# Gate and up of three feed-forward blocks as seven half-size products in place of eight, with the weights split in pieces of 512 words

## The reference, cut to what matters

```
def swiglu(x, w_gate, w_up, w_down):
    return (jax.nn.silu(x @ w_gate) * (x @ w_up)) @ w_down

h = h + 0.5 * swiglu(rms_norm_2(h, norm_ffn[layer, 0]), ffn_w_gate[layer, 0], ffn_w_up[layer, 0], ffn_w_down[layer, 0])
```

## Time and profile before

| | |
|---|---|
| median of 3 runs | 2825.6 us (2819.83 to 2830.66) |
| span of the profiled execution | 2823.2 us |
| TensorE busy | 2733.2 us, 97% |
| VectorE busy | 1312.7 us, 46% |
| ScalarE busy | 847.7 us, 30% |
| GpSimd busy | 562.7 us, 20% |
| DMA | 248.24 MB, 88 GB/s in the mean |

### The profile page before, as it was taken

How to read it: one execution, slowest core, us unless ns; L and a number is a source line. 1 busy time by engine, 2 the same in 40 slices (tenths; PEclk the granted TensorE clock), 3 DMA queues, 4 the chain that set the end, 5 groups by cost and what they waited for, 6 DMA issues and landing times. The chain is left out here.

```text
span 2823.2 us, 38779 instructions
## 1 busy us (share of the span) xinstructions
PE 2733.2 (97%) x16250; PEld 2191.5 (78%) x16250; DVE 1312.7 (46%) x1851; ACT 847.7 (30%) x1269; POOL 562.7 (20%) x387
## 2 busy tenths in 40 slices
PE   7999898999999999999999999999999999999998
PEld 5868755778888788888868888888888756888886
DVE  3454668453332643435455433454334566543433
ACT  3232135521212421213263221232222346421212
POOL 2000123422112230213201212122021100031202
PEclk8999989989999999999999999999999999999999
DMA  8250310123232233323203323233232240333221
GB/s 279 62 165 24 102 38 5 60 75 105 90 105 79 86 105 96 99 87 108 79 13 108 102 92 100 79 105 104 90 104 79 64 105 1 96 98 105 90 93 42
DMA packets 256942, 248.24 MB, mean 88 GB/s; under 512 B 25972, under 2 KB 252088, under 8 KB 256640
## 3 DMA queue, kind: packets, MB, share of 16 engines
q1 hardware_dynamic: 256562, 245.70, 27.8%
q10 hardware_dynamic: 206, 0.06, 0.0%
HBM read 241.52 MB, written 2.12 MB: 86 GB/s over the span
## 5 line engine op out<-in xcount | busy, mean ns | idle before, releaser
L537 DVE TENSOR_TENSOR dense_wt_lo<-ring,dense_wt_hi 128x2048 fp32r<-128x2048 f32 (+1 forms) x177 | 436.8, 2468 | 290.2 <-ACT dense_wt_hi L522 290.2
L522 ACT CAST dense_wt_hi<-ring 128x2048 fp32r<-128x2048 f32 (+1 forms) x177 | 328.1, 1854 | 758.9 <-PE bank L764 752.8
L1276 POOL TENSOR_TENSOR dense_act_hi<-dense_act,const 128x512 fp32r<-128x512 f32 x110 | 212.8, 1935 | 1307.2 <-DVE dense_act L1268 1307.2
L764 PE MATMUL bank<-feat_hi,dense_wt_hi 128*128 128x512 f32 x1344 | 414.6, 390 | 0.0
L764 PE MATMUL bank<-feat_hi,dense_wt_lo 128*128 128x512 f32 x1344 | 413.7, 389 | 0.0
L764 PE MATMUL bank<-feat_lo,dense_wt_hi 128*128 128x512 f32 x1344 | 413.7, 389 | 0.0
L764 PEld LDWEIGHTS bank<-feat_hi,dense_wt_hi 128*128 128x128 f32 x1344 | 252.3, 188 | 53.3 <-issue 1.0
L764 PEld LDWEIGHTS bank<-feat_lo,dense_wt_hi 128*128 128x128 f32 x1344 | 252.3, 188 | 52.4
L764 PEld LDWEIGHTS bank<-feat_hi,dense_wt_lo 128*128 128x128 f32 x1344 | 252.3, 188 | 52.4
L764 PE MATMUL bank<-dense_act_hi,dense_wt_hi 128*128 128x512 f32 x912 | 281.5, 390 | 1.0 <-POOL dense_act_lo L1278 0.9
L764 PE MATMUL bank<-dense_act_hi,dense_wt_lo 128*128 128x512 f32 x912 | 280.8, 389 | 0.0
(11 more groups left out here) (631 smaller groups left out, 3842.2 us busy)
## 6 DMA issues: line engine op xcount, KB each, us to landing
ring<-in_ffn_w_gate SPq DMA_DIRECT2D x44, 1024.0 KB, 5.4
ring<-in_ffn_w_up SPq DMA_DIRECT2D x44, 1024.0 KB, 5.4
ring<-in_ffn_w_down SPq DMA_DIRECT2D x32, 1024.0 KB, 5.0
ring<-in_ada_w SPq DMA_DIRECT2D x24, 1024.0 KB, 7.5
ring<-in_ffn_w_down SPq DMA_DIRECT2D x16, 768.0 KB, 4.2
...
```

What stands on the lines that cost most here:

```text
L522: self.nc.scalar.copy(self.wh[:, n % 2, 0:words], K.ring[:, n % RING, 0:words]).then_inc(K.high_done, 1)
L537: self.nc.vector.tensor_tensor(self.wl[:, n % 2, 0:words], K.ring[:, n % RING, 0:words], self.wh[:, n % 2, 0:words].bitcast(F32), ALU.subt ...
L764: lasts[m] = pe.matmul(outs[m], a, b, start=n == 0 and p == 0, stop=end and p == 2)
L1276: nc.gpsimd.tensor_tensor(ah[:, f, :], a[:, i % 2, :], K.k("ones")[:, 0:1].broadcast_to([P, T]), ALU.mult)
```

## The change

A unit is one tile of up and the same tile of gate. The weights of a unit are taken as a 2 x 2 matrix of blocks (a11, a12: up with feature tiles 0 to 3 and 4 to 7; a21, a22: gate with the same), the features as a 2 x 2 matrix (tiles 0 to 3 or 4 to 7 by tokens 0 to 255 or 256 to 511). In place of eight block products there are seven (Strassen, in Winograd's form), P1 to P7, each of four feature tiles by 256 tokens. Four sums of weight blocks are made by GpSimd in float32, partly in place in the ring (`sums_before`, `sum_first`, `sum_last`), four sums of feature blocks by GpSimd once a block (`NextOperands.pool`), and the results are put together by accumulation in PSUM and by short additions on VectorE and copies on ScalarE. A weight piece is now one block, 512 words, with six kept in `wh` and `wl` and split five ahead of TensorE. The high part of the hidden tile moves from GpSimd to ScalarE. Hidden tiles go in groups of 4, 6, 6 and 6. A unit's weights come as two DMAs with rows of 512 bytes where a chunk had one with rows of 1 KB, and a slot of the ring is given to the chunk that needs it next, in an order worked out in `Plan.place`. The output projections and the latent projection in front of and behind the blocks use the same pieces, with whole products of 512 tokens as before. The first two blocks of the program keep the old form.

```diff
+BLOCKS = 6
+LEAD = BLOCKS - 1
+BW = 4 * P
+HT = T // 2
+GROUPS = (4, 6, 6, 6)
+STARTS = (0, 4, 10, 16)
+OPERAND = {"P1": "b11", "P2": "b21", "P3": "b22", "P4": "t4", "P5": "t1", "P6": "t2", "P7": "t3"}
...
+    unit((0, "P1"), (0, "P5"), (1, "P1"), (1, "P5"), (0, "P2"), (1, "P2"), (0, "P6"), (1, "P6"), (0, "P7"), (1, "P7"),
+         (0, "P4"), (0, "P3"), (1, "P4"), (2, "P1"), (1, "P3"), (2, "P2"), (2, "P5"))
+    for u in range(2, KF - 1):
+        unit((u, "P6"), (u + 1, "P1"), (u, "P7"), (u + 1, "P2"), (u + 1, "P5"), (u, "P4"), (u, "P3"))
+        if u + 1 in STARTS:
+            g = STARTS.index(u + 1) - 1
+            n = GROUPS[g] // 2
+            for e in (0, 1):
+                for j in range(n - 1):
+                    down(g, e, j)
...
+class Blocks:
+    def __init__(self, K, st):
+        self.K, self.nc = K, K.nc
+        self.wh, self.wl = st.sb("wt_hi", [P, BLOCKS, BW], F32R), st.sb("wt_lo", [P, BLOCKS, BW], F32R)
+        self.sums = st.sb("wt_sum", [P, BW])
...
+                self.items.append({"P1": (n, part(0), None), "P2": (n, part(1), None), "P4": (n, part(3), None),
+                                   "P5": (n, self.sums[:, :], (self.s_s13, 2 * v + 1)), "P7": (n, part(2), (self.s_s13, 2 * v + 2)),
+                                   "P6": (n, part(0), (self.s_s2, v + 1)), "P3": (n, part(1), (self.s_s4, v + 1))}[p])
...
+    def high(self, act, i):
+        if i < len(self.items):
+            n, src, need = self.items[i]
+            if need:
+                act.wait_ge(*need)
+            else:
+                self.K.wait_loaded(act, n)
+            if i >= BLOCKS:
+                act.wait_ge(self.s_used, i - BLOCKS + 1)
+            self.nc.scalar.copy(self.wh[:, i % BLOCKS, :], src).then_inc(self.s_high, 1)
+    def low(self, dve, i):
+        if i < len(self.items):
+            dve.wait_ge(self.s_high, i + 1)
+            self.nc.vector.tensor_tensor(self.wl[:, i % BLOCKS, :], self.items[i][1], self.wh[:, i % BLOCKS, :].bitcast(F32),
+                                         ALU.subtract).then_inc(self.s_low, 1)
+    def sums_before(self, pool, u):
+        if u < len(self.units):
+            n, t = self.units[u][0], self.nc.gpsimd.tensor_tensor
+            a11, _, a21, a22 = (self.K.raw(n)[:, a * BW:(a + 1) * BW] for a in range(4))
+            self.K.wait_loaded(pool, n)
+            if u:
+                pool.wait_ge(self.s_low, self.units[u - 1][1][2] + 1)
+                pool.drain()
+            t(self.sums[:, :], a21, a22, ALU.add).then_inc(self.s_s13, 1)
+            pool.drain()
+            t(a21, a11, a21, ALU.subtract).then_inc(self.s_s13, 1)
+    def sum_first(self, pool, u):
+        if u < len(self.units):
+            n, (i1, _, _) = self.units[u]
+            a11 = self.K.raw(n)[:, 0:BW]
+            pool.wait_ge(self.s_low, i1 + 1)
+            pool.drain()
+            self.nc.gpsimd.tensor_tensor(a11, self.sums[:, :], a11, ALU.subtract).then_inc(self.s_s2, 1)
+    def sum_last(self, pool, u):
+        if u < len(self.units):
+            n, (_, i2, _) = self.units[u]
+            s2, a12 = (self.K.raw(n)[:, a * BW:(a + 1) * BW] for a in range(2))
+            pool.wait_ge(self.s_low, i2 + 1)
+            pool.drain()
+            self.nc.gpsimd.tensor_tensor(a12, a12, s2, ALU.subtract).then_inc(self.s_s4, 1)
+    def product(self, pe, i, out, feats, start, rows=range(4), stop=True, shared=False):
+        h, l = self.wh[:, i % BLOCKS, :], self.wl[:, i % BLOCKS, :]
+        for k in rows:
+            xh, xl = feats(k)
+            w = slice(k * P, (k + 1) * P)
+            pe.matmul(out, h[:, w], xh, start=start and k == 0, stop=False, skip_group_check=shared)
+            pe.matmul(out, h[:, w], xl, start=False, stop=False, skip_group_check=shared)
+            last = pe.matmul(out, l[:, w], xh, start=False, stop=stop and k == 3, skip_group_check=shared)
+        return last
...
+    def pool(self, pool, q):
+        t = self.nc.gpsimd.tensor_tensor
+        f, f4 = self.f[q % 2], self.f4[q % 2]
+        if q:
+            pool.wait_ge(self.s_lo, 6 * (q - 1) + 4)
+        pool.wait_ge(self.s_f, 2 * q + 1)
+        t(self.t1, f[:, HT:T], f[:, 0:HT], ALU.subtract).then_inc(self.s_t, 1)
+        pool.drain()
+        pool.wait_ge(self.s_f, 2 * q + 2)
+        t(self.t2, f4[:, HT:T], self.t1, ALU.subtract).then_inc(self.s_t, 1)
+        t(f[:, HT:T], f4[:, HT:T], f[:, HT:T], ALU.subtract).then_inc(self.s_t, 1)
+        pool.drain()
+        pool.wait_ge(self.s_lo, 6 * q + 1)
+        t(f[:, 0:HT], f4[:, 0:HT], self.t2, ALU.subtract).then_inc(self.s_t, 1)
...
+    end = [max(place[step] for step in order if step[:3] == ("down", len(GROUPS) - 1, e)) for e in range(4)]
+    tiles = lambda e: (e, e + 4) if operands else (2 * e, 2 * e + 1)
+    bank = lambda e, m: K.bank[4 + 2 * (e % 2) + m][:, :]
+    lo, hi = slice(0, HT), slice(HT, T)
+    group = lambda u: [g for g in range(len(GROUPS)) if STARTS[g] <= u][-1]
+    a = lambda u: K.bank[2 * (u % 2)][:, lo]
+    b = lambda u: K.bank[2 * (u % 2)][:, hi]
+    c = lambda u: K.bank[2 * (u % 2) + 1][:, lo]
+    scaled = {place["unit", u, "P3"] + 1: u for u in range(KF)}
+    split = {place["unit", u, "P3"] + 2: u for u in range(KF)}
...
+        def unit(n, u, p, rows=range(4)):
+            o = OPERAND[p]
+            if u < 2:
+                pe.wait_ge(now.s_lo, now.ready(o, rows[-1]))
+            if 0 in rows:
+                pe.wait_ge(B.s_low, base + n + 1)
+                if p == "P1" and u >= 2:
+                    pe.wait_ge(s_e4, u - 1)
+                elif p == "P5" and u >= 2:
+                    pe.wait_ge(s_e5, u - 1)
+                elif p == "P6":
+                    pe.wait_ge(s_e1, u + 1)
+                elif p == "P7":
+                    pe.wait_ge(s_u2, u + 1)
+                elif p in ("P4", "P3"):
+                    pe.wait_ge(s_e3, u + 1)
+            out = {"P2": b, "P5": c, "P3": c}.get(p, a)(u)
+            last = B.product(pe, base + n, out, lambda k: sec.operand(o, k), p in ("P1", "P5"), rows, shared=True)
+            if 3 in rows:
+                last.then_inc(B.s_used, 1)
...
+            B.high(act, base + n + LEAD)
+            if n == 0:
+                now.scalar_first(act, 3, prev.done)
...
+            if n in split:
+                u = split[n]
+                f = u - STARTS[group(u)]
+                act.wait_ge(s_act, u + 1)
+                nc.scalar.copy(sec.act_hi[:, f, :], sec.gate[:, u % 2, :]).then_inc(s_ah, 1)
+            if step[0] == "unit" and step[2] == "P2":
+                u = step[1]
+                if u >= 2:
+                    act.wait_ge(s_act, u - 1)
+                act.wait_ge(B.s_used, base + n + 1)
+                nc.scalar.copy(sec.up[:, u % 2, lo], b(u)).then_inc(s_b, 1)
+            if step[0] == "unit" and step[2] == "P6":
+                u = step[1]
+                if u >= 2:
+                    act.wait_ge(s_al, u - 1)
+                act.wait_ge(B.s_used, base + place["unit", u, "P5"] + 1)
+                nc.scalar.copy(sec.gate[:, u % 2, hi], c(u)).then_inc(s_c, 1)
+                act.wait_ge(B.s_used, base + n + 1)
+                if u >= 2:
+                    act.wait_ge(s_e5, u - 1)
+                nc.scalar.copy(sec.u2[:, u % 2, :], a(u)).then_inc(s_u2, 1)
+            if step[0] == "unit" and step[2] == "P3":
+                u = step[1]
+                act.wait_ge(s_gate, u + 1)
+                nc.scalar.activation(sec.gate[:, u % 2, :], sec.gate[:, u % 2, :], ACT.Silu).then_inc(s_silu, 1)
...
+            B.low(dve, base + n + LEAD)
...
+            if n in scaled:
+                u = scaled[n]
+                g = sec.gate[:, u % 2, :]
+                dve.wait_ge(s_silu, u + 1)
+                v.tensor_tensor(g, g, K.rs[:, :], ALU.mult)
+                dve.drain()
+                v.tensor_tensor(g, g, sec.up[:, u % 2, :], ALU.mult).then_inc(s_act, 1)
...
+            if step[0] == "unit":
+                u, p = step[1], step[2]
+                up, gate = sec.up[:, u % 2, :], sec.gate[:, u % 2, :]
+                if p in ("P7", "P4", "P3"):
+                    dve.wait_ge(B.s_used, base + n + 1)
+                if p == "P2":
+                    dve.wait_ge(s_b, u + 1)
+                    v.tensor_tensor(up[:, lo], a(u), up[:, lo], ALU.add).then_inc(s_e1, 1)
+                elif p == "P7":
+                    dve.wait_ge(s_c, u + 1)
+                    v.tensor_tensor(gate[:, hi], a(u), gate[:, hi], ALU.add).then_inc(s_e3, 1)
+                elif p == "P4":
+                    if u == 0:
+                        dve.wait_ge(now.s_rs, 1)
+                    v.tensor_tensor(gate[:, lo], a(u), K.rs[:, lo], ALU.mult).then_inc(s_e4, 1)
+                    dve.drain()
+                    v.tensor_tensor(gate[:, hi], gate[:, hi], K.rs[:, hi], ALU.mult).then_inc(s_gate, 1)
+                elif p == "P3":
+                    dve.wait_ge(s_u2, u + 1)
```

(40 more changed lines are left out.)

628 lines of the change are left out of this document (513 added, 115 removed).

## The result

The changed kernel takes 2921.3 us (median of 4 runs) against 2822.7 (4 runs beside it): a ratio of 1.0349, 95% interval 1.0325 to 1.0372. It is slower by some 99 us; the forecast was slower by 55, and its range ended at 2910.

The account below looks back on a forecast made before the run. TensorE's product count times spacing bound the kernel; after the change, VectorE would, through exclusion with GpSimd. Per block -17.5 (arithmetic) + 37.5 (waits) - 1.6 (present start loss) = +18.4; three: +55 on 2825.6, giving 2881 us, range 2790 to 2910.

Parts of the forecast that it names:

- slow units: Third to fifth or later units of a group, past the split lead: some 12.4 us each instead of 10.1.
- 0.120 us a product and 10.08 us a unit: TensorE in the changed blocks: 84 products of 256 columns a unit, against 10.88 us before; gain 0.80 us a unit.
- nothing for ScalarE and the DMA: In a unit, ScalarE's 6.6 us and the DMA's 6.3 fit under TensorE; DMA up to some 2 us at block starts.
- The step-through: Four engine queues stepped in order, first come, first served: cycle of 12.4 us, 8.9 us lost per group of six.
- some 110: Sign to look for: TensorE's waits in the changed blocks, in us in all, put down to VectorE and ScalarE operations.
- 2.0 us until the third operand's sum exists: At a block's start: loss while ScalarE's copy of that operand stands behind a split awaiting the first product.
- some 8.8 in the first group: First group of a block: us lost as GpSimd also queues sums of operands and squares ahead of the weights'.
- rival (2): Changed blocks: TensorE stays the bound, units stay at 10.1 us, total 2775 to 2800 us; chance 0.18.
- -52.6 + 3 x 2: Three changed blocks with TensorE as bound: arithmetic gain of 52.6 us less 2 us for each block's start.
- (4) *Heavier: Changed blocks: no unit is spared and the start is dearer, over 2910, up to 2945 us; chance 0.08.
- hold: Exclusive time of a GpSimd operation, in which VectorE's two-SBUF-input operations are shut out: 1.08 us each.
- VectorE's 7.2 us a unit: VectorE's own work in a changed unit, 4.4 us before; alone it would fit under TensorE's 10.08.

Follow-up runs that it names:

- e1: Changed kernel with GpSimd's four sums of weights per unit cut to 8 of 512 words (first sum of a section whole): 2804.7 us, ratio 0.9953.
- e7: Changed kernel with GpSimd's four sums of weights replaced by fills with zero of the same 512 words: 2807.6 us, ratio 0.9958.
- e9: Changed kernel with each GpSimd sum of weights replaced by three fills with zero, drains between: 2812.9 us, ratio 0.9986.
- e10: Changed kernel with each GpSimd sum of weights replaced by a copy of one 512-word operand: 2814.0 us, ratio 0.9990.
- e3: Changed kernel with both the sums of weights and the start's operand sums and squares cut to 8 words: 2796.3 us, ratio 0.9938.
- e2: Changed kernel with GpSimd's operand sums and squares at the blocks' starts cut to 8 words, sums of weights whole: 2898.8 us, ratio 1.0299.
- e4: Changed kernel with GpSimd making each hidden tile's low part twice, a drain between: 2943.4 us, ratio 1.0450.
- e5: Changed kernel with all four sums of weights moved from GpSimd to VectorE, each behind a drain: 2907.3 us, ratio 1.0306.
- e8: Changed kernel with the four sums of weights on VectorE at the end of a step, without drains ahead of them: 2851.5 us, ratio 1.0123.

## Why the prediction was right and wrong

**Right: the direction and, for the slow units, the mechanism.** VectorE's operations on two SBUF tiles and GpSimd's on two SBUF tiles wait for each other, whole, and this turns a gain into a loss. e1, e7, e9 and e10 leave TensorE's, ScalarE's and VectorE's work as it is and bring every unit of the groups of six to 10.08 us; e9 excludes GpSimd's lateness there. The prediction cited the Trainium skill (SBUF — State Buffer, Who interferes with whom), by which a VectorE instruction with two SBUF inputs contends with a GpSimd instruction that reads SBUF, and not with one that only writes. The sums agree with the first half (low parts of 1129 ns) and e9's fills, which only write, with the second (791). e10 does not fit the first half: its copies read SBUF, and the low parts took 808 ns where the copies beside them took 871 for 620. Here the measurement decides: a copy with one input gave way and held VectorE up little.

**Right: 0.120 us a product and 10.08 us a unit**, and nothing for ScalarE and the DMA. The first two units of each group of six run at 10.08 and 10.45. By the formula for an isolated product in the Trainium skill (TensorE: Matmul & The Clock Gate, Back-to-back issue gap) it would have been 0.109 us, an estimate; the changed kernel shows 0.120 wherever TensorE does not wait and has its full clock, so the measured figure stands.

**Right: the steady state.** The step-through gave 12.4 us a slow unit and 8.9 lost in a group of six. It is 12.68 and 9.9, the last group 7.4: 27.2 us a block where the forecast had 26.7. TensorE's waits came to 108 us in all against "some 110", on the operations named, but that they agree is in part luck: the forecast's figure was all that the stretches lose, and they lose 147 us. The waits listed leave out the small gaps around each wait, the norm's products and the products at half clock.

**Wrong: the block's start**, "2.0 us until the third operand's sum exists" and "some 8.8 in the first group". The two terms, 10.8 us a block, measured 20.0, 27.0 and 18.8 (64.6, 71.6 and 63.4 less 44.6): 33 us more in three blocks. With the 1.5 us more in the other groups that makes 90 of the 94 us by which the blocks grew, against the 55 forecast. The distances between product starts (what exceeds 0.12 us) divide the 65.8 us of the three blocks: 22.6 in waits for the last rows of features and operands; 20.6 in the wait for `up` ahead of P6 of the third unit, 6.9 in each block; 12.8 in 138 products at half clock; some 10 in the norm's products, the first two units' P6 and small gaps. The runs tell what caused them:
- The order by itself, with nothing in VectorE's way, loses 8.2 a block (e3), not 2.0: waits for `up` in P6, the features' last row, the norm's products (1.6, there before as well), products at half clock (1.8). This took 19 us from the gain of rival (2), whose "-52.6 + 3 x 2" would give -47 before its "some for the first group": e3 stands at -22.
- The sums of weights add 5.9, 7.6 and 6.4 (e2 less e3). The wait for `up` in the third unit is 5.7 us in e2 and 1.9 in e3, as in e1.
- The squares and the operands' sums add nothing in the first and third block as long as no weight sums run, 8.2 in the second (e1 less e3).
- Together they add 11.5, 18.9 and 10.7 (changed kernel less e3). The second block is dearest, probably since its operands are made while the first block's last outputs are added.

The step that failed is the stepping through the first group. I had priced the start by GpSimd's queue, as a delay of the weights' sums. Missed was what stands behind the stretched operations on VectorE. At the edge that is the addition into x, on which ScalarE's scaling, the features and all the rest depend; it came 4.7 us after the last product. In the third unit it is the addition into `up`, the largest single loss of each first group. And the sum kept TensorE at full clock, so the slower products stood at nothing: in the first block the clock fell to 0.50 within the wait of 2.8 us and again within that of 6.7, and in all three blocks this cost the 12.8 us. The exclusion was applied to the units in steady state, not to the start.

**Wrong in size: the upper range.** It stopped at 2910 because (4) *Heavier* was built of slow units, with the start as a remark. The start had been given no bounds of its own, and they should have set the width.

**The theory's own limit** showed in e4 and e5. I then treated a hold as a term that adds to the unit; it adds only what reaches the wait that ends last (0.41 of 1.08). And VectorE's 7.2 us a unit plus four sums was put at 10.0, where it came to 11.4: four drains at 0.17 make half of the difference, and the hidden tile's low part on GpSimd, which still held one of VectorE's (1.37 us in e8's timeline against 0.68), about the rest.
